# A hybrid decoder layer on one core: two column groups of eight banks become pairs of four banks, with other TensorE work between their matmuls

## The chip, the cores and the metric

The kernel runs on one core of one Trainium2 chip (trn2). The metric is the device time of one execution in microseconds (us), as the median of several runs. TensorE is shortened to PE in the profile, VectorE to DVE, ScalarE to ACT, GpSimd to POOL and SyncE to SP.

## The reference

One layer of a decoder for a prompt of 256 rows and samples of 8 x 4 rows, all float32, 288 rows in all:

```python
x = x + 0.5 * _swiglu(_rmsnorm(x, g_ffn1), w1_gate, w1_up, w1_down)
h = _rmsnorm(x, g_mix)
proj = h @ w_in      # q_a, k_a, v_a, f_a | qk_m (2048), v_m (1024), o_m (1024) | i_m, f_m
...                  # forgetting attention on q_a, k_a, v_a, with cached pages for the samples
qk_c = silu(causal_conv(qk_m))
h_m, C, n, m = _mlstm(q_m, k_m, v_m, i_pre, log_f_m, C0, n0, m0)
y_m = sigmoid(o_m) * _rmsnorm(h_m, g_out_m)
x = x + concatenate([y_a, y_m]) @ w_out
x = x + 0.5 * _swiglu(_rmsnorm(x, g_ffn2), w2_gate, w2_up, w2_down)
```

The output gate o_m is needed only after the mLSTM heads. Besides x, the states and the new keys and values go out.

## The kernel before

Activations lie transposed: a feature tile of 128 on the partitions, the 288 rows along the free axis. Each weight matrix is read once. Each value is split in two float32r parts, and a product of two tiles is three matmuls of 288 columns: hi x hi, lo x hi, hi x lo (L1786 to L1788, "products" below).

Work runs in groups. A group is up to eight column tiles of 128, one in each PSUM bank, summed over all k tiles. The k tiles come in turns of four slots of w_raw, w_hi and w_lo. TensorE takes a turn in two steps, slots 0 and 1, then 2 and 3: each is 48 products at eight banks. SP loads a slot as soon as its last contents are split. ScalarE casts it to w_hi (L632) once TensorE has used that slot of the turn before (w_used), VectorE subtracts for w_lo (L1010), and TensorE waits for w_lo of both slots of a step. At a group's end VectorE drains the banks one by one (banks_free), and the next group's first matmul on a bank waits for that. Each engine has its order written out by hand.

Between products a group can carry other TensorE work in free banks: turn_products calls between(step, b) behind each bank. The group in_a (six banks) does so.

The projection for the mLSTM heads is in_m, four groups of eight banks and four turns: q, k, v, gate. Beside the third and fourth, VectorE computes the causal convolutions (conv, L1543 to L1547, two tiles a turn, two places in conv_acc) and ScalarE their silu (L902):

```python
split_pair(g.turn + 2 * g.turns + (t + 1), 0, width)   # ScalarE, turn t
conv_silu(2 * t)
conv_silu(2 * t + 1)
...
if j >= 2:                                             # VectorE, conv(j)
    dve.wait_ge(sem("conv_used"), 2 * (j - 1))
```

Behind the fourth group comes the heads' preparation: TensorE spreads the samples' decay rows (L2161), transposes v (L1979), two gate rows (L2168) and k (L2186), lays the samples' k and v out by sequence (by_sequence, L2175), computes head 0's scores (L2202 to L2209), transposes the convolution's last rows (L2217), and takes the samples' scores (L2222) and a spread row (L2226). ScalarE and VectorE copy the results out and take the gate's sigmoid (L926). Then the loop over eight heads starts (L2241 is its first matmul). Its states come from DRAM in a ring of four places, two of them slots of w_raw.

The last group is the second half of the second SwiGLU's down projection, down1b: two groups of eight banks and five turns. Behind it, 48 transposes (L2337) turn the result to rows, ScalarE and VectorE copy (L993, L1762), and POOL stores three pieces (L551).

Of the kernel before, what the change touches and what calls it, by code (L numbers as in the profile page):

```python
# [31 lines left out]
F32 = mybir.dt.float32  # L32
# [46 lines left out]
def plan():  # L79
# [17 lines left out]
def build(nc, A, O):  # L97
# [77 lines left out]
    with scope:  # L175
        r_("ym_top", [P, 512])
        ym_hi, ym_lo = r_("ym_hi", [P, H, T], F32R), r_("ym_lo", [P, H, T], F32R)
    right_side, r_ = area("right")
    kmn = r_("kmn", [P, 2, H * HD])
    kms = r_("kms", [P, H * HD])  # L180
    v_seq = r_("v_seq", [P, H, 2, HD])
    C = r_("C", [P, 2, NB, HD])
    Ws, qw, qn = r_("Ws", [SM, H, SM]), r_("qw", [P, H, 2, SM]), r_("qn", [P, H, SM])
    Wt = r_("Wt", [P, 2, 384])
    Cp = r_("Cp", [P, 2, HD])


    kws, vws = qn, Cp[:, :, :].rearrange("p r (h s) -> p (r h) s", s=SM)
    C_ring = [C[:, 0, :, :], C[:, 1, :, :]] + [w_raw[:, i, :].rearrange("p (b e) -> p b e", b=NB) for i in (2, 3)]
# [15 lines left out]
    with scope_mixer:  # L205
# [40 lines left out]
        with scope:  # L246
# [7 lines left out]
            counts = l_("counts", [P, TP])  # L254
            k_sums = l_("k_sums", [P, H, NB])
# [29 lines left out]
    G_A, G_M, G_O = groups["in_a"].index, groups["in_m"].index, groups["out_a"].index  # L285
    OUT_A, OUT_B, OUT_M = groups["out_a"], groups["out_b"], groups["out_m"]
# [24 lines left out]

    def x_final(eng, i, t):
# [4 lines left out]
        else:  # L317
            g = groups["down0b" if i == 1 else "out_m"]
            eng.wait_ge(banks_free, NBANK + g.index * NBANK + t + 1)

# [7 lines left out]
    def _(sp):  # L328
# [18 lines left out]
        def load_swiglu(n):  # L347
# [3 lines left out]
            def down(k0, col):  # L351
                return lambda k: [(0, wd[n][k + k0, :, bass.ds(col, UW)])]
# [14 lines left out]
            g = groups[f"down{n}b"]  # L367
            with sp.Fori(0, 2) as i:
# [28 lines left out]

        def load_out():
# [3 lines left out]
            load_turn(a.turn, range(SLOTS), columns(wo, 0, a.width))  # L402
            load_turn(a.turn + 1, range(2), lambda s: columns(wo, 0, a.width)(SLOTS + s))
# [56 lines left out]
        def state_traffic():  # L460


            sp.wait_ge(banks_free, NBANK + G_O * NBANK)

            def load_state(h):
                sp.dma_start(C_ring[h % 4], A["state_C"][0, :, h, :, :].rearrange("b d e -> d b e")).then_inc(
                    sem(f"C_loaded{h % 4}"), 16)

# [3 lines left out]
            load_state(0)  # L472
# [18 lines left out]
        load_mixer("in_m", 4, wi, COL_M, load_pages)  # L491
# [12 lines left out]
    def _(pool):  # L504
# [79 lines left out]
        pool.wait_ge(banks_free, NBANK + G_O * NBANK)  # L584
        nc.gpsimd.memset(qw[:, :, :, :], 0.0).then_inc(sem("km_ready"), 1)
# [6 lines left out]

        pool.wait_ge(sem("o_sigmoid"), 1)
        for h in range(H):
            pool.wait_ge(sem("sq_ready"), SUM_M + h + 1)
# [7 lines left out]
        for t, n in TT:  # L603
            pool.wait_ge(sem("y_rows_ready"), 2 * (t + 1))
            pool.wait_ge(sem("y_rows_ready_v"), 2 * (t + 1))
            if t < 2:
                store(O["y_prompt"][0, t * P:(t + 1) * P, :], y_rows[:, t, :])
            else:
                store(O["y_sample"].rearrange("b t d -> (b t) d"), y_rows[0:SM, 2, :])
        pool.wait_ge(out_stored, 16 * (6 + 4 + 2 + 3))  # L610
# [1757 lines left out]
```

## Time and profile before

| | |
|---|---|
| runs | 2315.3 us median of 3 (2314.76 to 2317.62) |
| the profiled execution | 2320.72 us, span 2319.1 us |
| TensorE busy | 2290.2 us, 99% |
| VectorE, ScalarE, POOL busy | 53%, 36%, 2% |
| mean granted TensorE clock | 0.994 |
| DMA | 384 MB, 166 GB/s on the mean |

Times in rows are us from the span's start. A timeline row has start, duration, engine, line, operation, output and inputs, and in brackets the idle time before it and who ended it. Matmuls overlap, so the distance of starts tells the pace, not the duration. A plain float32 matmul is counted twice. A windows row has the stretch, its length, then busy us of PE, its weight loads, DVE, ACT and POOL, the granted clock as a share of 2.4 GHz, the DMA share and GB/s.

### The profile page before, as it was taken

How to read it: one execution, taken by the hardware profiler on the slowest of the kernel's cores; microseconds unless marked ns; L12 is line 12 of the kernel's file. 1: busy time of each engine (PE TensorE's matmuls, PEld its weight loads, DVE VectorE, ACT ScalarE, POOL GpSimd, SP SyncE). 2: the span in 40 equal slices, each digit the busy share in tenths (PEclk: the TensorE clock that was granted, in tenths of full speed). 3: DMA queues.
4: the chain of work that ended last, by engine and by line, in shares of the span. 5: the costliest groups of instructions: out<-in, count | busy, mean ns of one | idle time of the engine just before them, and what ended most of it. 6: DMA issues, size and time to landing. Idle time of an engine off the chain costs nothing.

```text
span 2319.1 us, 48002 instructions
## 1 busy us (share of the span) xinstructions
PE 2290.2 (99%) x17805; PEld 2246.8 (97%) x17805; DVE 1228.4 (53%) x1907; ACT 842.8 (36%) x1109; POOL 50.3 (2%) x84
## 2 busy tenths in 40 slices
PE   9999999999999999999999999999999999999998
PEld 8999999999999999887999989999999999999997
DVE  6554444355444455467456766755554434554443
ACT  4333333333333343334334433533333333333332
POOL 2000000000000010010000110000000000000000
PEclk9999999999999999999999999999999999999999
DMA  6555555555554444547445455455554445555443
GB/s 169 180 166 164 164 164 175 166 166 163 171 166 166 165 152 146 168 136 271 157 164 167 132 155 173 151 181 163 163 163 168 171 168 169 168 164 168 164 163 131
DMA packets 176901, 384.05 MB, mean 166 GB/s; under 512 B 19133, under 2 KB 44853, under 8 KB 176501
## 3 DMA queue, kind: packets, MB, share of 16 engines
q1 hardware_dynamic: 173888, 375.99, 50.4%
q0 software_dynamic: 2512, 5.57, 0.8%
q10 hardware_dynamic: 416, 1.32, 0.2%
q8 instruction: 58, 0.95, 0.2%
q14 instruction: 27, 0.22, 0.0%
HBM read 373.09 MB, written 9.70 MB: 165 GB/s over the span
## 4 chain that ended last, share of the span: by engine, by line
PE 95%; DVE 3%; ACT 1%; DMA 0%; issue 0%; SPq 0%; POOL 0%; ACTq 0%; DVEq 0%; POOLq 0%
PE ps L1788 30%; PE ps L1786 30%; PE ps L1787 29%; DVE w_lo L1010 1%; PE ps L2044 1%; DMA w_raw<-in_w_up 0%; ACT w_hi L632 0%; PE ps L2057 0%; PE ps L1856 0%; PE ps L1857 0%; PE ps L1863 0%; PE ps L1990 0%; PE ps L2337 0%; PE ps L1979 0%; PE ps L2245 0%
## 5 line engine op out<-in xcount | busy, mean ns | idle before, releaser
L1010 DVE TENSOR_TENSOR w_lo<-w_raw,w_hi 128x1024 fp32r<-128x1024 f32 (+2 forms) x698 | 789.7, 1172 | 983.9 <-ACT w_hi L632 982.5
L632 ACT CAST w_hi<-w_raw 128x1024 fp32r<-128x1024 f32 (+2 forms) x698 | 670.6, 1008 | 1290.3 <-PE ps L1788 1284.7
L1786 PE MATMUL ps<-x_hi,w_hi 128*128 128x288 f32 (+1 forms) x2752 | 813.0, 295 | 4.4 <-DVE w_lo L1010 2.6
L1788 PE MATMUL ps<-x_hi,w_lo 128*128 128x288 f32 (+1 forms) x2752 | 813.9, 296 | 0.0
L1787 PE MATMUL ps<-x_lo,w_hi 128*128 128x288 f32 (+1 forms) x2752 | 807.7, 293 | 0.0
L1786 PEld LDWEIGHTS ps<-x_hi,w_hi 128*128 128x128 f32 x2752 | 517.5, 188 | 6.3 <-DVE w_lo L1010 3.0
L1787 PEld LDWEIGHTS ps<-x_lo,w_hi 128*128 128x128 f32 x2752 | 521.2, 189 | 0.1
L1788 PEld LDWEIGHTS ps<-x_hi,w_lo 128*128 128x128 f32 x2752 | 516.5, 188 | 0.0
L1786 PE MATMUL ps<-hid_hi,w_hi 128*128 (+1 forms) x1376 | 405.6, 295 | 1.4 <-DVE X L1243 1.4
L1788 PE MATMUL ps<-hid_hi,w_lo 128*128 (+1 forms) x1376 | 407.0, 296 | 0.0
L1787 PE MATMUL ps<-hid_lo,w_hi 128*128 (+1 forms) x1376 | 403.8, 293 | 0.0
L1786 PE MATMUL ps<-xm_hi,w_hi 128*128 128x288 f32 (+1 forms) x896 | 267.6, 299 | 2.5 <-DVE w_lo L1010 2.1
L1788 PE MATMUL ps<-xm_hi,w_lo 128*128 128x288 f32 (+1 forms) x896 | 266.2, 297 | 0.0
L1787 PE MATMUL ps<-xm_lo,w_hi 128*128 128x288 f32 (+1 forms) x896 | 262.1, 293 | 0.0
L1787 PEld LDWEIGHTS ps<-hid_lo,w_hi 128*128 128x128 f32 x1376 | 260.6, 189 | 0.0
L1786 PEld LDWEIGHTS ps<-hid_hi,w_hi 128*128 128x128 f32 x1376 | 258.7, 188 | 1.9 <-DVE X L1243 1.9
L1788 PEld LDWEIGHTS ps<-hid_hi,w_lo 128*128 128x128 f32 x1376 | 258.2, 188 | 0.0
L1786 PEld LDWEIGHTS ps<-xm_hi,w_hi 128*128 128x128 f32 x896 | 168.8, 188 | 7.0 <-DVE w_lo L1010 3.4
L1787 PEld LDWEIGHTS ps<-xm_lo,w_hi 128*128 128x128 f32 x896 | 171.3, 191 | 0.1
L1788 PEld LDWEIGHTS ps<-xm_hi,w_lo 128*128 128x128 f32 x896 | 168.5, 188 | 0.0
L747 ACT ACTIVATE gate<-gate 128x288 f32<-128x288 f32 x86 | 38.3, 445 | 57.5 <-DVE gate L1187 57.5
L1191 DVE TENSOR_TENSOR up<-ps,rsx 128x288 f32<-128x288 f32 x86 | 38.6, 449 | 8.0 <-PE ps L1788 8.0
(487 smaller groups left out, 1438.1 us busy)
## 6 DMA issues: line engine op xcount, KB each, us to landing
w_raw<-in_w_down SPq DMA_DIRECT2D x178, 512.0 KB
w_raw<-in_w_gate SPq DMA_DIRECT2D x320, 256.0 KB
w_raw<-in_w_up SPq DMA_DIRECT2D x320, 256.0 KB
w_raw<-in_w_in SPq DMA_DIRECT2D x64, 512.0 KB
w_raw<-in_w_in SPq DMA_DIRECT2D x64, 384.0 KB
page<-in_cache_k SPq DMA_DIRECT2D x16, 512.0 KB, 4.6
w_raw<-in_w_out SPq DMA_DIRECT2D x16, 512.0 KB
w_raw<-in_w_gate SPq DMA_DIRECT2D x32, 192.0 KB
```

The source lines that it names most:

```text
L632: nc.scalar.copy(w_hi[:, slot, 0:width], w_raw[:, slot, 0:width]).then_inc(w_hi_ready, 1)
L747: nc.scalar.activation(gate[:, j, :], gate[:, j, :], ACT.Silu).then_inc(sem("silu_ready"), 1)
L1010: nc.vector.tensor_tensor(w_lo[:, slot, 0:width], w_raw[:, slot, 0:width], w_hi[:, slot, 0:width].bitcast(F32), ALU.subtract).then_inc(w_l ...
L1191: nc.vector.tensor_tensor(up[:, j, :], ps[:, 2 * j + 1, 0:T], rsx[:, :], ALU.mult).then_inc(banks_free, freed)
L1786: mm(out, hi, x_hi[:, k, :], start=first and pair == 0 and s == slots[0], stop=False)
L1787: mm(out, hi, x_lo[:, k, :], start=False, stop=False)
L1788: ins = mm(out, lo, x_hi[:, k, :], start=False, stop=last and pair == 1 and s == slots[-1])
L2044: ins = tr(ps[:, 5 + 2 * half, i * P:(i + 1) * P], page[:, p % 3, c:c + HD], ident[:, :])
```

## The change

in_m keeps three groups. The gate's 1024 columns become in_o, two groups of four tiles (width 512, four turns each), and the heads' preparation runs between their products in banks 4 to 7. Only scores(0) stays behind them. ScalarE's and VectorE's parts of it are laid out by step. The convolutions move up by a group, to 0, 2, 3, 3 tiles in the turns of the second group and two in each turn of the third. The gate's sigmoid is in two halves, the second behind head 0's exponentials. POOL computes qw. SBUF buffers on the right side get new places, and SP issues the first state load earlier, behind the third turn of in_o's second group.

The second group of down1b becomes down1c, two groups of four tiles and five turns each. Transposes of the eight column tiles already done run between the first one's products, those of the next four between the second one's, and 12 are left behind. The rows go out in nine stores, three of 512 columns at the end from SP and ScalarE. SP's two idle loads at the end are gone.

```diff
@@ -84,9 +84,11 @@
     gate_up_c = [c for j in range(3) for c in (j * P, 384 + j * P)]
     swiglu = [("gu{}c", 1, KD, KD, gate_up_c), ("gu{}a", 5, KD, KD, gate_up), ("down{}a", 2, 24, CHUNK, plain),
               ("gu{}b", 5, KD, KD, gate_up), ("down{}b", 2, 20, 20, plain)]
-    mixer = [("in_a", 4, KD, KD, plain[:6]), ("in_m", 4, KD, KD, plain),
+    mixer = [("in_a", 4, KD, KD, plain[:6]), ("in_m", 3, KD, KD, plain),
+             ("in_o", 2, KD, KD, plain[:4]),
              ("out_a", 1, H, H, plain[:6]), ("out_b", 2, H, H, plain[:5]), ("out_m", 2, H, H, plain)]
-    for n, part in ((0, swiglu), (0, mixer), (1, swiglu)):
+    ending = swiglu[:-1] + [("down{}b", 1, 20, 20, plain), ("down{}c", 2, 20, 20, plain[:4])]
+    for n, part in ((0, swiglu), (0, mixer), (1, ending)):
         for name, count, nk, real, tiles in part:
             out[name.format(n)] = Group(turn, index, nk, real, tiles)
...
@@ SBUF, right side
...
+    kws, vws = (xt[:, i, 0:H * SM].rearrange("p (h s) -> p h s", s=SM) for i in range(2))
+    C_ring = [C0[:, :, :], C1[:, :, :]] + [w_raw[:, i, :].rearrange("p (b e) -> p b e", b=NB) for i in (2, 3)]
     def swiglu_memory(n):
...
+    def conv_tiles(t):
+        first = (0, 0, 2, 5)[t] if t < 4 else 2 * t
+        return range(first, (0, 2, 5, 8)[t] if t < 4 else first + 2)
     def x_final(eng, i, t):
...
@@ SyncE
+        def load_state(h):
+            sp.dma_start(C_ring[h % 4], A["state_C"][0, :, h, :, :].rearrange("b d e -> d b e")).then_inc(
+                sem(f"C_loaded{h % 4}"), 16)
+
         def load_out():
             load_turn(a.turn, range(SLOTS), columns(wo, 0, a.width))
+            sp.wait_ge(w_used, O_MOST)
+            load_state(0)
             load_turn(a.turn + 1, range(2), lambda s: columns(wo, 0, a.width)(SLOTS + s))
             state_traffic()
...
-        for s in range(2):
-            sp.wait_ge(w_loaded[s], 32 * (n_turns + 1))
+        for u in (9, 11):
+            sp.wait_ge(sem("y_rows_ready_v"), u // 2 + 1)
+            sp.dma_start(*y_part(u % 3, 3, 4)).then_inc(sem("y_stored"), 16)
 
 
     SUM_QK, SUM_Y, SUM_M = 0, 16, 24
...
@@ GpSimd
+        for x in qw:
+            nc.gpsimd.memset(x[:, :, :], 0.0).then_inc(sem("km_ready"), 1)
+        pool.wait_ge(sem("km_ready"), H + 2)
+        pool.wait_ge(sem("s_all_ready"), 2)
+        for i in range(2):
+            half = slice(16 * i, 16 * (i + 1))
+            ins = nc.gpsimd.tensor_tensor(qw[i][:, :, half], ext[:, 0:H, TP + 16 * i:TP + 16 * (i + 1)], s_all[:, :, 0, half],
+                                          ALU.mult)
+        ins.then_inc(sem("qw_ready"), 1)
+
         pool.wait_ge(sem("o_sigmoid"), 1)
         for h in range(H):
...
+            pool.wait_ge(sem("y_rows_ready"), (1, 3, 2)[t])
+            pool.wait_ge(sem("y_rows_ready_v"), (2, 1, 3)[t])
+            store(*y_part(t, 0, 2))
+        for t in range(3):
+            pool.wait_ge(sem("y_rows_ready_v" if t == 1 else "y_rows_ready"), (6 + t) // 2 + 1)
+            store(*y_part(t, 2, 3))
+        pool.wait_ge(out_stored, 16 * (6 + 4 + 2 + 6))
+        pool.wait_ge(sem("y_stored"), 3 * 16)
         for b in range(4):
             pool.wait_ge(sem(f"C_stored{b}"), 16 * (H // 4))
         for b in range(2):
...
@@ ScalarE
         for t in range(2 * g.turns):
-            width = UW if t < 2 * g.turns - 1 else OUT_A.width
-            split_pair(g.turn + 2 * g.turns + (t + 1), 0, width)
-            conv_silu(2 * t)
-            conv_silu(2 * t + 1)
-            split_pair(g.turn + 2 * g.turns + (t + 1), 2, width)
...
+        def sigmoid(i):
+            act.wait_ge(banks_free, NBANK + (IN_O.index + i + 1) * NBANK)
+            nc.scalar.activation(om[:, 4 * i:4 * i + 4, :], om[:, 4 * i:4 * i + 4, :], ACT.Sigmoid).then_inc(sem("o_sigmoid"), 1)
+        def conv_rows_copy(b):
+            act.wait_ge(sem("conv_rows_done"), b + 1)
+            nc.scalar.copy(conv_rows[:, b * 512:(b + 1) * 512], ps[0:27, (7, 4, 5, 6)[b], :]).then_inc(sem("conv_rows_ready"), 1)
+        def split_o(step):
+            split_pair(IN_O.turn + step // 2, step % 2 * 2, IN_O.width if step < 16 else OUT_A.width)
+        for step in range(16):
+            if step >= 1:
+                split_o(step + 1)
+            if step == 0:
                 act.wait_ge(sem("conv_used"), 2 * 2 * H)
-            nc.scalar.copy(s_all[:, 4 * b:4 * b + 4, :, :], ps[:, 6 + b, 0:384].rearrange(
-                "p (h r s) -> p h r s", h=4, r=3)).then_inc(sem("s_all_ready"), 1)
-        for i in range(4):
-            act.wait_ge(sem("vT_done"), 6 + i + 1)
-            nc.scalar.copy(vmn[:, i // 2, 4 * (i % 2):4 * (i % 2) + 4, 0:HD],
-                           ps[:, i, :].rearrange("p (h d) -> p h d", h=4)).then_inc(sem("vn_ready"), 1)
-        nc.scalar.activation(om[:, :, :], om[:, :, :], ACT.Sigmoid).then_inc(sem("o_sigmoid"), 1)
-        for i in range(2):
-            act.wait_ge(sem("kmsT_done"), i + 1)
-            nc.scalar.copy(kms[:, i * 512:(i + 1) * 512], ps[:, 4 + i, :]).then_inc(sem("kms_ready"), 1)
...
+            if step == 9:
+                sigmoid(0)
+            if step == 10:
+                act.wait_ge(sem("ws_logits"), 1)
+                nc.scalar.activation(Ws, Ws, ACT.Exp).then_inc(sem("ws_exp"), 1)
+            if step == 15:
+                act.wait_ge(w_used, O_MOST)
+                for i in range(2):
+                    act.wait_ge(sem("kmsT_done"), i + 1)
+                    nc.scalar.copy(kms[:, i * 512:(i + 1) * 512], ps[:, 7 - 2 * i, :]).then_inc(sem("kms_ready"), 1)
+        split_o(17)
         def e_exp(h):
...
+        def y_copy(u):
+            act.wait_ge(sem("y_rows_done"), u + 1)
+            (t, n), q = TT[u % 3], u // 3
+            nc.scalar.copy(y_rows[0:n, t, q * 512:(q + 1) * 512], ps[0:n, 4 + u % 4, :]).then_inc(sem("y_rows_ready"), 1)
+        g = groups["down1c"]
+        for kt in range(1, 2 * g.turns):
+            split_pair(g.turn + kt, 0, g.width)
+            if kt == g.turns + 2:
+                y_copy(6)
+            if kt == g.turns + 3:
+                y_copy(8)
+            split_pair(g.turn + kt, 2, g.width)
+            if kt <= 3:
+                y_copy(2 * kt - 2)
+        y_copy(10)
+        act.wait_ge(sem("y_rows_ready"), 10 // 2 + 1)
+        act.dma_start(*y_part(1, 3, 4)).then_inc(sem("y_stored"), 16)
...
@@ VectorE
@@ -1547,14 +1627,15 @@
                     nc.vector.scalar_tensor_tensor(acc, src, w, acc, ALU.mult, ALU.add).then_inc(sem("conv_done"), 1)
 
         g = groups["in_m"]
-        for i in range(4):
-            if i < 2:
-                split_turns(g, g.turn + i * g.turns, g.turns, UW)
+        for i in range(3):
+            width = UW if i < 2 else IN_O.width
+            if i == 0:
+                split_turns(g, g.turn, g.turns, UW)
             else:
                 for t in range(g.turns):
-                    conv((i - 2) * H + 2 * t)
-                    conv((i - 2) * H + 2 * t + 1)
-                    split_pair(g.turn + i * g.turns + (t + 1), 0, UW if (i, t) != (3, g.turns - 1) else OUT_A.width)
+                    for j in conv_tiles((i - 1) * g.turns + t):
+                        conv(j)
+                    split_pair(g.turn + i * g.turns + (t + 1), 0, UW if t < g.turns - 1 else width)
                     if t < g.turns - 1:
                         split_pair(g.turn + i * g.turns + (t + 1), 2, UW)
...
+        for step in range(16):
+            if step >= 1:
+                split_o(step + 1)
+            if step == 0:
...
+            if step == 6:
+                dve.wait_ge(sem("spread_done"), 2 * H + 1)
...
+            if step == 7:
+                in_o_out(0)
+            if step == 11:
+                dve.wait_ge(sem("ws_exp"), 1)
+                dve.wait_ge(sem("ws_scores"), 1)
...
+            if step == 12:
+                dve.wait_ge(w_used, O_HALF)
+                v_apart(0)
+                k_weighted(0)
+            if step == 13:
+                k_weighted(1)
+                v_apart(1)
+            if step == 14:
+                k_weighted(2)
+                k_weighted(3)
+        in_o_out(1)
+        split_o(17)
...
@@ TensorE
+        def beside_o1(step, b):
+            if step == 0 and b == 2:
+                s_spread()
+            if step == 1 and b < 2:
+                v_natural(b, 4 + b)
+            if step == 2 and b < 2:
+                pe.wait_ge(sem("s_all_ready"), b + 1)
+                v_natural(2 + b, 6 + b)
+            if step == 3 and b < 2:
+                pe.wait_ge(sem("vn_ready"), 6 + b + 1)
+                v_natural(4 + b, 4 + b)
...
+            if step == 6 and b == 0:
+                pe.wait_ge(sem("km_ready"), H)
+                pe.wait_ge(sem("conv_rows_ready"), 1)
+                for h in range(H):
+                    ins = mm(ps[0:SM, 7, h * SM:(h + 1) * SM], ext[:, H + h, TP:T], ext[:, h, TP:T], start=True, stop=True)
+                ins.then_inc(sem("ws_scores"), 1)
+            if step == 6 and b == 1:
+                pe.wait_ge(sem("root_ready"), 2)
+                pe.wait_ge(sem("conv_rows_ready"), 2)
+                mm(ps[:, 4, 0:TP], ones[0:H, :], sq[0:H, 0, 0:H * SM], start=True, stop=True).then_inc(sem("spread_done"), 1)
+        def beside_o2(step, b):
+            if step == 2 and b == 0:
+                pe.wait_ge(sem("vws_ready"), 1)
+                pe.wait_ge(sem("ya_scaled"), 1)
+                by_sequence(vws, 0, 4, "vsT_done")
+            if step == 2 and b == 1:
+                pe.wait_ge(sem("conv_rows_ready"), 3)
+                by_sequence(vws, 1, 5, "vsT_done")
+            if step == 3 and b == 0:
+                pe.wait_ge(sem("conv_rows_ready"), 4)
+                k_natural(0, 6)
+            if step == 4 and b == 0:
+                pe.wait_ge(sem("ws_ready"), 1)
+                k_natural(1, 7)
...
+            if step == 6 and b == 0:
+                pe.wait_ge(sem("kws_ready"), 1)
+                pe.wait_ge(sem("kw_ready"), 2)
+                by_sequence(kws, 0, 7, "kmsT_done")
+            if step == 6 and b == 2:
+                pe.wait_ge(sem("v_seq_ready"), 2)
+                by_sequence(kws, 1, 5, "kmsT_done")
+        for i, beside in ((0, beside_o1), (1, beside_o2)):
+            for kt in range(IN_O.turns):
+                turn_products(IN_O, IN_O.turn + i * IN_O.turns, IN_O.index + i, kt, xm_hi, xm_lo, kt == 0,
+                              kt == IN_O.turns - 1, xr, beside)
...
-                pe.wait_ge(sem("kw_ready"), 2)
+                pe.wait_ge(banks_free, G_O * NBANK + 2)
...
+        def y_transposes(u):
+            (t, n), q = TT[u % 3], u // 3
+            pe.wait_ge(banks_free, (g.index if u < 6 else g.index + 1 if u < 9 else g.index + 2) * NBANK + NBANK)
+            if u >= 4:
+                pe.wait_ge(sem("y_rows_ready" if u % 2 == 0 else "y_rows_ready_v"), (u - 4) // 2 + 1)
             for j in range(4):
-                ins = tr(ps[0:n, i % 4, j * P:(j + 1) * P], X[:, (i % 4) * 4 + j, t * P:t * P + n], ident[:, :])
+                ins = tr(ps[0:n, 4 + u % 4, j * P:(j + 1) * P], X[:, q * 4 + j, t * P:t * P + n], ident[:, :])
             ins.then_inc(sem("y_rows_done"), 1)
+        def beside_first(step, b):
+            if 1 <= step <= 6 and b == 3:
+                y_transposes(step - 1)
+        def beside_second(step, b):
+            if 2 <= step <= 4 and b == 3:
+                y_transposes(step + 4)
+        for i, beside in ((0, beside_first), (1, beside_second)):
+            for kt in range(g.turns):
+                turn_products(g, g.turn + i * g.turns, g.index + i, kt, *mem[1]["hid"], kt == 0, kt == g.turns - 1, hr, beside)
+        for u in range(9, 12):
+            y_transposes(u)
     ctx.close()
```

## Rows read from the trace of the kernel before

**Rows 1.** The page's chain that ended last, share of the span by engine.

```profile
PE 95%; DVE 3%; ACT 1%; DMA 0%; issue 0%; SPq 0%; POOL 0%; ACTq 0%; DVEq 0%; POOLq 0%
```

**Rows 2.** Windows: busy us (x instructions) of each engine, granted clock, DMA.

```profile
1310.82:1317.65 6.83, 6.83 (x36) 5.80 (x34) 2.96 (x8) 4.63 (x8) 0.00 (x0) 0.50 1.15 296
1368.87:1375.70 6.83, 6.83 (x33) 6.68 (x33) 1.84 (x6) 0.42 (x1) 1.30 (x3) 0.50 0.44 135
2303.05:2308.50 5.45, 5.45 (x48) 5.00 (x48) 3.44 (x5) 3.31 (x6) 1.03 (x2) 1.00 0.22 92
```

**Rows 3.** Timeline of TensorE, heads' preparation: start us, us, line, operation.

```profile
1308.42 0.29 PE L1787 MATMUL ps<-xm_lo,w_hi 128*128 128x288 f32 x1
1308.55 0.29 PE L1788 MATMUL ps<-xm_hi,w_lo 128*128 128x288 f32 x1
1309.40 2.46 PE L2161 MATMUL ps<-s_rows,sel 8*128 8x96 f32 x16 [0.55 <-DVE om L1570]
1311.78 5.38 PE L1979 MATMUL ps<-ident,vm 128*128 128x128 f32 x24
...
1317.67 1.06 PE L2175 MATMUL ps<-ident,Cp 128*8 128x128 f32 x32
1318.66 1.97 PE L2186 MATMUL ps<-ident,ext 128*128 128x128 f32 x16
...
1323.29 0.70 PE L2202 MATMUL ps<-ext 128*128 128x256 f32 x2
...
1324.68 1.91 PE L2217 MATMUL ps<-ident,conv_last 128*27 128x128 f32 x16
...
1328.17 0.49 PE L2241 MATMUL ps<-vmn,kmn 128*128 128x129 f32 x2
```

**Rows 4.** Chain that ended last: the third head's scores, start us, us.

```profile
1334.93 0.63 PE ps L2202 x2
```

**Rows 5.** Timelines of ScalarE, then VectorE, in a turn with two convolutions.

```profile
1215.77 1.28 ACT L902 ACT_TABLE_LOAD   x1
1217.06 0.51 ACT L902 ACTIVATE ext<-conv_acc,vecs 128x256 f32<-128x256 f32 x1
...
1220.09 2.00 ACT L632 CAST w_hi<-w_raw 128x1024 fp32r<-128x1024 f32 x2 [1.69 <-PE ps L1788]
1226.43 2.00 ACT L632 CAST w_hi<-w_raw 128x1024 fp32r<-128x1024 f32 x2 [4.34 <-PE ps L1788]
1228.34 0.50 ACT L902 ACTIVATE ext<-conv_acc,vecs 128x256 f32<-128x256 f32 x1
...
1223.45 0.38 DVE L1543 TENSOR_SCALAR conv_acc<-ext,vecs 128x312 f32<-128x312 f32 x1
...
1227.52 2.36 DVE L1010 TENSOR_TENSOR w_lo<-w_raw,w_hi 128x1024 fp32r<-128x1024 f32 x2
```

**Rows 6.** Timeline of TensorE: plain fp32 matmuls between products.

```profile
928.17 0.29 PE L1788 MATMUL ps<-xm_hi,w_lo 128*128 128x288 f32 x1
928.40 1.14 PE L1863 MATMUL ps<-xt,one_hot 128*8 128x288 f32 x4
...
929.71 0.29 PE L1787 MATMUL ps<-xm_lo,w_hi 128*128 128x288 f32 x1
```

**Rows 7.** Timeline of the end of the span, all engines.

```profile
2302.20 0.29 PE L1788 MATMUL ps<-hid_hi,w_lo 128*128 128x288 f32 x1
...
2303.05 5.46 PE L2337 MATMUL ps<-ident,X 128*128 128x128 f32 x48 [0.55 <-DVE X L1243]
...
2308.55 0.68 DVE L1762 COPY y_rows<-ps 32x512 f32<-32x512 f32 x1 [0.19 <-PE ps L2337]
2309.79 0.51 POOL L551 DMA_DIRECT2D out_y_sample<-y_rows  x1 [1.19 <-DVE y_rows L1762]
```

**Rows 8.** DMA issues: queue, count, KB each, median us to landing.

```profile
out_C_prompt<-Cp SPq DMA_DIRECT2D x8, 64.0 KB, 3.1
...
out_y_sample<-y_rows POOLq DMA_DIRECT2D x1, 256.0 KB, 4.5
```

More of the change, by code:

```diff
@@ L285, in build @@
     G_A, G_M, G_O = groups["in_a"].index, groups["in_m"].index, groups["out_a"].index
+    IN_O = groups["in_o"]
+    O_HALF, O_MOST = ((IN_O.turn + IN_O.turns + n) * 2 + 2 for n in (2, 3))
     OUT_A, OUT_B, OUT_M = groups["out_a"], groups["out_b"], groups["out_m"]
@@ L367, in load_swiglu @@
             g = groups[f"down{n}b"]
+            if n == 1:
+                load_group(g, g.turn, down(CHUNK, 0))
+                g = groups["down1c"]
+                with sp.Fori(0, 2) as i:
+                    load_group(g, i * g.turns + g.turn, down(CHUNK, i * g.width + UW, g.width))
+                return
             with sp.Fori(0, 2) as i:
@@ L644, in split_pair, with split_groups @@
             split_hi(turn, s + 1, width)
-        def split_groups(g, n, after, last=False):
+        def split_groups(g, n, after):
             split_turns(g, g.turn, n * g.turns, after)
-            if not last:
-                split_pair(g.turn + n * g.turns, 2, after)
+            split_pair(g.turn + n * g.turns, 2, after)
         def square(i, src):
@@ L945, in _ @@
         e_exp(0)
-        for b in range(4):
-            act.wait_ge(sem("conv_rows_done"), b + 1)
-            nc.scalar.copy(conv_rows[:, b * 512:(b + 1) * 512], ps[0:27, 2 + b, :]).then_inc(sem("conv_rows_ready"), 1)
-        act.wait_ge(sem("ws_logits"), 1)
-        nc.scalar.activation(Ws[:, :, :], Ws[:, :, :], ACT.Exp).then_inc(sem("ws_exp"), 1)
+        sigmoid(1)
         for h in range(H):
@@ L2163, in _, with s_spread @@
-        natural(lambda h, c, n: vm[:, h, c:c + n], 0, "vT_done")
-        pe.wait_ge(sem("rows_exp"), 3)
-        pe.wait_ge(sem("s_all_ready"), 1)
-        for a, row in enumerate((r_row, ws_row)):
-            for t, n in TT:
-                ins = tr(ps[0:n, 6, (3 * a + t) * H:(3 * a + t + 1) * H], row[:, t * P:t * P + n], ident[0:H, 0:H])
-        ins.then_inc(sem("nat_done"), 1)
-        def by_sequence(src, bank, made):
+        def s_spread():
+            pe.wait_ge(banks_free, NBANK + IN_O.index * NBANK)
+            pe.wait_ge(sem("s_rows_ready"), 1)
+            for b in range(2):
+                for j in range(4):
+                    ins = mm(ps[:, 6 + b, j * 96:(j + 1) * 96], sel[0:H, 4 * b + j, :].bitcast(F32), s_rows[:, :, :],
+                             start=True, stop=True)
+                ins.then_inc(sem("s_all_done"), 1)
@@ new lines, in v_natural, with rows_natural @@
+        def v_natural(i, bank):
+            (t, n), half = TT[i // 2], i % 2
+            for j in range(4):
+                ins = tr(ps[0:n, bank, j * P:(j + 1) * P], vm[:, 4 * half + j, t * P:t * P + n], ident[:, :])
+            ins.then_inc(sem("vT_done"), 1)
+        def rows_natural():
+            for a, row in enumerate((r_row, ws_row)):
+                for t, n in TT:
+                    ins = tr(ps[0:n, 6, (3 * a + t) * H:(3 * a + t + 1) * H], row[:, t * P:t * P + n], ident[0:H, 0:H])
+            ins.then_inc(sem("nat_done"), 1)
@@ new lines, in conv_natural, with k_natural, by_sequence @@
+        def conv_natural(i, bank):
+            for j in range(4):
+                ins = tr(ps[0:27, bank, j * P:(j + 1) * P], conv_last[:, 4 * i + j, :], ident[:, :])
+            ins.then_inc(sem("conv_rows_done"), 1)
+        def k_natural(i, bank):
+            for j in range(4):
+                ins = tr(ps[:, bank, j * P:(j + 1) * P], ext[:, H + 4 * (i % 2) + j, i // 2 * P:(i // 2 + 1) * P], ident[:, :])
+            ins.then_inc(sem("kT_done"), 1)
+        def by_sequence(src, i, bank, made):
```

297 lines of the change are left out of this document (156 added, 141 removed).

## The prediction, made before the kernel ran

> **What bounds the kernel now.** I read the page first: the chain that ended last runs through TensorE for 95% of the span [rows 1], and the engine's busy share is 99%. So a change can save only three things: TensorE standing idle, TensorE at its lower clock, and what follows its last instruction. Moving TensorE work from one place to another saves nothing by itself, since it stays on the same engine. I then asked for the granted clock of short windows round the two places that the change touches [rows 2], and last for the order of time there [rows 3 to 7] and the landing times of DMAs [rows 8].
>
> The windows show two stretches of 6.83 us with TensorE busy throughout and a clock of 0.50, the level of 1.2 GHz: one inside the heads' preparation, one behind the heads' loop [rows 2]. What ran before the first was a wait of 0.7 us for the last bank and then matmuls with 8 weight rows (L2161). Each costs 3.4 us.
>
> **The heads' preparation, before.** The last product of the gate's group starts at 1308.55, so the next would be due at 1308.68 (products start 0.13 apart). The heads' loop starts at 1328.17 (L2241) [rows 3]. That is 19.5 us between them. At 2.4 GHz the moved instructions take:
> - 16 matmuls L2161: 2.4 us, 0.9 of it at the lower clock, so 1.9
> - 24 transposes of v (L1979): 48 transposes took 5.47 us [rows 7], 0.114 each, so 2.7. They took 5.3 here
> - six small transposes 0.3
> - four calls of by_sequence: 1.0 for the first (1317.67 to 1318.66) and the same for the last. The 2.74 us from the end of the 16 k transposes (L2186, 1.9 us) to L2202 hold the last and the two for k, so 1.7 for those two, 3.7 in all
> - 16 k transposes 1.8 and 16 of the conv rows 1.8
> - sample scores and the spread of ya's roots, out of the 3.5 us from L2217 to L2241: 0.9
>
> Sum 13.1 us. scores(0) stays where it was: from L2202 at 1323.29 to L2217 at 1324.68, 1.4. So 19.5 is 13.1 + 1.4 + 3.4 of lower clock + some 1.6 of waits.
>
> **The heads' preparation, after.** The 13.1 us now stand between products. What does a switch cost? Two plain fp32 matmuls between products took 1.54 us from the start of the product before to the second one after. Less 2 x 0.13 for the products and 1.07 for themselves, 0.2 is left [rows 6]. Seven pieces of that kind give 1.4. For transposes I take nothing, their engine order is the same as in the stretch of 48. Lower bound of the switches 0, upper 0.2 for each of some 20 pieces, 4.0.
>
> Behind the last product: VectorE must first split 768 columns for two slots and then drain four banks. A pair of 1024 takes ScalarE 2.00 and VectorE ends some 3.4 us behind ScalarE's start [rows 5]. With 768 I estimate 2.9 from the start of the last step, itself 3.2 long, and 0.4 to 0.5 a drain. scores(0) waits for two banks: 0.7 us after the last product. It takes 1.4, and the loop starts at 2.1, since all banks are free at 1.4. Sum after: 13.1 + 1.4 + 2.1 = 16.6. **Gain 19.5 less 16.6, 2.9 us.**
>
> Do the products wait in the new groups? A step is now 24 products, 3.16 us, in place of 6.35. For 512 columns I estimate 1.2 us for ScalarE's two casts and 0.7 for VectorE's last subtraction: half the 1024 rows and a little more [rows 5]. With 0.3 of signal the weights are ready 2.2 us into a step of 3.16 or more. I went through the 16 steps: the longest extra work on either engine (ScalarE's gate for four tiles, with its table 2.4 us; VectorE's v_apart and k_weighted, 1.9) stands in or before steps that inserted work has lengthened by 0.4 to 2 us. I find no wait. What POOL has to do (two memsets, two multiplications) is over some 5 us before the loop asks. The first state load is issued at the end of the fourteenth step, 8 us ahead of the loop; the 256 KB store behind two larger ones landed in 4.5 us [rows 8], so 512 KB should do in well under 8. The second gate's sigmoid now stands on ScalarE between the first and second head, with a table load before and after: 1.3 + 1.1 + 1.3. By my order of time head 1's exponentials end 7.4 us after the last product, and VectorE has multiplied them at 7.9. TensorE asks for them in scores(2), which starts 6.8 us after the loop [rows 3, 4], so at 8.9. Cover 1.0 us, cost nothing.
>
> The Trainium skill (ScalarE: Activation LUTs, section What ACT_TABLE_LOAD costs) gives each switch a drain of 1.38 us on top of the load's 1.28. With two switches TensorE would wait 1.8 us there, and this part's gain would be 1.1. But the activation that follows the load of 1215.77 starts at 1217.06 [rows 5]: 1.28 and no drain, so the sum goes without it.
>
> **The convolutions, moved earlier.** They now stand in two groups, no longer beside the gate's, as 0, 2, 3, 3 tiles in the first one's turns and 2, 2, 2, 2 in the second's. I find the costliest side effect here. Two tiles take VectorE 4.07 us (1223.45 to 1227.52) [rows 5]. Both places of conv_acc are in use, so the third tile of a turn waits for ScalarE's silu of the first. ScalarE's program puts that behind the cast of the next turn's slots 0 and 1, and the cast waits until half of the turn is done. In times from the turn's start (1219.83 in [rows 5]): cast 6.6 to 8.5, silu to 9.2, third conv 9.3 to 11.3, VectorE's two subtractions to 13.6. TensorE wants them at 12.7. So it waits 1.0 us, in two turns. In the second of them the drain of eight banks comes after, and bank 0 is free only 0.5 later: 1.4 us. **Cost 2.4 us.** Lower bound 0, if the order is looser than I read; upper 4, if two waits also shift the turn behind them.
>
> **The last eight column tiles.** Before: the last product starts at 2302.20, the next would be due at 2302.33, and the span ends at 2319.1, 16.8 us later. In it are one drain (to 2303.05), 48 transposes 5.5, the copy of 0.7 from 2308.55, the store issued at 2309.79, landing 4.5 us later at 2314.3 [rows 7, 8], and 4.8 us to the end of the span, which I take as fixed. After: 36 transposes stand between products, nine pieces of 0.44 to 0.46, 4.0 us, still on TensorE. Behind the last product: drain 0.7, 12 transposes, of which the last four end at 2.1, copy from 2.3 to 3.0, a store of 64 KB from SP with 3.1 to land [rows 8] ends at 6.1, then 4.8: 10.9. 16.8 less 10.9 less 4.0: **gain 1.9 us.** Bounds 0.9 (a landing of 4.1) and 2.9 (2.1). The removed dummy loads at the end lie on SP under products and save nothing. Of the ten turns, each step is again 3.16 us against a chain of 2.2; the copies of y rows, 0.6 to 0.7, fit in the 0.9 left and the 0.4 that the inserted transposes add.
>
> **Sum.** 2.9 - 2.4 + 1.9 = 2.4 us off. From the profiled execution's own 2320.7 (span 2319.1): 2318.3. That execution is 5.4 us above the median of the runs, so I carry the difference over: 2315.3 - 2.4 = **2312.9 us**. A change under 0.2% (4.6 us) can't be told from none here.
>
> **The rivals.**
> 1. *No wait in the convolutions' turns.* Against it is the semaphore's order above, for it that TensorE idles nowhere in these groups before. Gain 4.8, time 2310.5. Chance 0.20.
> 2. *The second stretch at 1.2 GHz goes as well,* because the loop's tail falls otherwise in time. For it: it costs 3.4 us [rows 2]; against it: nothing in that tail's work changes. Gain 5.8, time 2309.5. Chance 0.12.
> 3. *The clock falls beside the preparation too.* For it: the 8-row matmuls L2161 preceded the fall, and now the convolutions' waits come close before. Against it: products now surround all of it, and they run at 1.00. The gain of 2.9 becomes -0.5, time 2316.3. Chance 0.12. The Trainium skill (TensorE: Matmul & The Clock Gate, section Part 4: PE-mode transpose) says that transposes don't count as activity for the clock, which would speak for this one. But 48 transposes in a row ran at 1.00 [rows 2].
> 4. *Slower: weights come late in the four-bank groups.* A slot's load is now issued 5 us before its cast is due, where it had some 11. 256 KB landed in 4.5 us behind two larger stores [rows 8], so they should fit, and 1 us of slack lies behind. The price: 18 turns, so 0.1 us late beyond that is 1.8 us. From 0.4 late it turns the sign past 0.2%: 7.2 less 2.4, 2320.1. Chance 0.10.
> My forecast 0.46. Its own range is 2309.5 to 2316.
>
> Faster by over 0.2% (below 2310.7) takes rival 1, rival 2 and a little of the forecast: 0.33. Slower (above 2319.9) is rival 4: 0.10. The rest is 0.57. Range 2307 to 2318: it leaves out rival 4 and the far ends of the others.
>
> **What would show it.** Right: from the last product of the gate to the heads' loop it is 2 to 3 us, with the clock at 1.00 beside the preparation. TensorE idles about 1.0 and 1.4 us in the second and third quarter of the convolutions' first group, released by w_lo. The last product to the span's end is about 11 us. Wrong: idle time of the products on w_lo or on a DMA in each four-bank turn, a clock of 0.50 there, or an end of the span that follows the last landing by other than 4.8 us.

## The result, and the profile after

The changed kernel takes 2320.95 us (median of 14 runs, 2318.02 to 2324.32), the kernel before 2317.59 in as many runs beside it (2314.76 to 2319.6): ratio 1.0018, 95% interval 1.0011 to 1.0025. That is 4.2 us slower (2.5 to 5.8), where I had forecast 2.4 us faster and a range up to 2318. It is just under the 0.2% that I called no change, but the interval leaves zero out, so the sign was wrong. Against the forecast's 2312.9 it is 8.0 us more, and 2.3 of them lie in the starting point: I took the median of 3 runs of the kernel before, 2315.3, where 14 give 2317.59. The profiled execution took 2324.32 us, span 2322.4.

The chain still runs through TensorE, but a DMA now has a share in it (compare [rows 1]).

```profile
PE 94%; DVE 3%; DMA 1%; ACT 1%; issue 1%; SPq 0%; ACTq 0%; DVEq 0%
```

I cut both traces at the same instructions and compared the parts, in us. The first part begins at the last transposes ahead of in_m. Parts 2, 3 and 6 are the change's own. "Lost" is what the lower clock took in parts 1 and 2, summed over slices as (1 - clock) x length.

| part | before | changed | difference |
|---|---|---|---|
| 1: to the gate's last product | 204.3 | 228.5 | +24.2 |
| 2: last product to heads' loop | 19.6 | 2.1 | -17.5 |
| 3: heads' loop to out_a | 44.9 | 44.6 | -0.3 |
| 4: out_a to SwiGLU's last x product | 802.2 | 802.4 | +0.2 |
| 5: from there to the last product | 126.9 | 131.4 | +4.5 |
| 6: last product to the span's end | 16.9 | 10.7 | -6.2 |
| lost to the lower clock in 1 and 2 | 3.4 | 3.4 | 0 |

So the end does what it should, and the front, which was to give 2.9 and take 2.4, costs 6.6. The waits of TensorE on the changed kernel, first in the convolutions' two groups, then round the second group of in_o:

```profile
PE ps L1923 <- DVE ext L1646: 1.3, 1, 1.3
PE ps L1923 <- DVE w_lo L1089: 0.8, 1, 0.8
...
PE ps L1923 <- DVE w_lo L1089: 3.2, 1, 3.2
```

The first two are the convolutions' waits of my step, 2.1 us together. The third I had nowhere. Its place in the timeline (POOL, ScalarE, TensorE):

```profile
1284.60 0.61 POOL L581 DMA_DIRECT2D out_conv_prompt<-conv_rows  x1 [27.59 <-ACT conv_rows L965]
1285.19 0.55 POOL L581 DMA_DIRECT2D out_conv_sample<-conv_rows  x1
1285.73 0.51 POOL L581 DMA_DIRECT2D out_m_prompt<-m_row  x1
1286.23 0.64 POOL L581 DMA_DIRECT2D out_m_sample<-m_row  x1
...
1296.65 0.62 ACT L674 CAST w_hi<-w_raw 128x512 fp32r<-128x512 f32 x1 [5.32 <-DMA w_raw<-in_w_in]
1298.21 1.85 ACT L674 CAST w_hi<-w_raw 128x512 fp32r<-128x512 f32 x3 [0.94 <-DMA w_raw<-in_w_in]
...
1299.61 0.61 PE L1923 MATMUL ps<-xm_hi,w_hi 128*128 128x288 f32 x1 [3.17 <-DVE w_lo L1089]
```

Read it from below: the second group's weights are 3.2 us late because ScalarE waited for two loads of in_w_in, and shortly before, POOL had issued four stores. They used to stand at the heads' loop and came forward together with the conv rows that they wait for. The chain of waits goes the same way: SP issues the load at 1287.01, and it ends at 1298.21.

```profile
1287.01 0.36 SPq L360
1287.67 10.51 DMA w_raw<-in_w_in
1298.21 0.63 ACT w_hi L674
1298.86 0.70 DVE w_lo L1089
```

The windows (columns as in [rows 2]) show what was slow, and what came of it:

```profile
1284.50:1287.00 2.50, 2.50 (x31) 2.30 (x30) 0.98 (x2) 1.14 (x2) 2.27 (x4) 1.00 0.80 243
1287.00:1296.00 9.00, 9.00 (x66) 8.51 (x65) 3.58 (x8) 1.14 (x2) 0.00 (x0) 1.00 0.88 57
1296.00:1299.60 3.60, 0.44 (x4) 0.20 (x2) 1.43 (x3) 2.00 (x4) 0.00 (x0) 0.92 0.62 182
1299.60:1306.10 6.50, 6.49 (x28) 6.50 (x29) 1.19 (x2) 3.18 (x4) 0.00 (x0) 0.52 0.51 156
```

For 9 us the DMA engines are 88% busy and move 57 GB/s, against 243 just before. TensorE idles, and still in the idle time the clock falls to the level of 1.2 GHz. Finer windows, from the same trace:

```profile
1298.00:1299.00 1.00, 0.00 (x0) 0.00 (x0) 0.14 (x1) 0.79 (x2) 0.00 (x0) 1.00 0.52 199
1299.00:1299.60 0.60, 0.00 (x0) 0.00 (x0) 0.60 (x2) 0.59 (x2) 0.00 (x0) 0.51 0.61 85
1299.60:1305.85 6.25, 6.24 (x26) 6.25 (x27) 1.19 (x2) 2.93 (x4) 0.00 (x0) 0.50 0.53 163
1305.85:1307.00 1.15, 1.15 (x22) 0.99 (x25) 0.52 (x1) 1.13 (x3) 0.00 (x0) 1.00 0.00 0
```

The stretch is 6.83 us long, as in [rows 2], and 6.25 of it fall on matmuls: 3.1 us lost. The issues of this stretch, with median us to landing:

```profile
out_conv_sample<-conv_rows POOLq DMA_DIRECT2D x1, 192.0 KB, 2.7
out_conv_prompt<-conv_rows POOLq DMA_DIRECT2D x1, 24.0 KB, 2.1
out_m_prompt<-m_row POOLq DMA_DIRECT2D x1, 0.0 KB, 4.8
out_m_sample<-m_row POOLq DMA_DIRECT2D x1, 0.2 KB, 9.5
```

The large stores land in 2 to 3 us; m_sample, 64 single elements of 4 bytes, needs 9.5.

The heads' part behind the last product (compare [rows 3]), and the end (compare [rows 7]):

```profile
1331.11 0.29 PE L1925 MATMUL ps<-xm_hi,w_lo 128*128 128x288 f32 x1
1331.80 0.70 PE L2418 MATMUL ps<-ext 128*128 128x256 f32 x2 [0.40 <-DVE om L1675]
...
1333.19 0.44 PE L2444 MATMUL ps<-vmn,kmn 128*128 128x129 f32 x2
...
2311.67 0.29 PE L1925 MATMUL ps<-hid_hi,w_lo 128*128 128x288 f32 x1
...
2312.59 1.53 PE L2544 MATMUL ps<-ident,X 128*128 128x128 f32 x12 [0.62 <-DVE X L1884]
...
2314.16 0.68 DVE L1876 COPY y_rows<-ps 32x512 f32<-32x512 f32 x1 [0.18 <-PE ps L2544]
...
2314.86 0.35 SPq L527 DMA_DIRECT2D out_y_sample<-y_rows  x1
```

scores(0) starts 0.7 behind the last product and the loop 2.1, the two figures of the forecast. The end is 10.7 (2322.4 less 2311.67) for 10.9. Two of its terms were off and cancel in part: the last store, issued at 2314.86, lands after 2.4 us where I had 3.1, and the span ends 5.1 behind that landing where I had 4.8.

### The profile page after: what moved, and what is told of

It is laid out like the page before. It is cut to its first block, busy times and chain, and to the rows that moved or that the text cites. A ratio compares the mean times of both kernels' runs of the same rounds, so it can differ in the third digit from the quotient of the medians.

```text
span 2322.4 us, 48173 instructions
## 1 busy us (share of the span) xinstructions
PE 2291.3 (99%) x17805; PEld 2246.5 (97%) x17805; DVE 1230.7 (53%) x1939; ACT 849.1 (37%) x1146; POOL 54.1 (2%) x90
## 4 chain that ended last, share of the span: by engine, by line
PE 94%; DVE 3%; DMA 1%; ACT 1%; issue 1%; SPq 0%; ACTq 0%; DVEq 0%
PE ps L1923 29%; PE ps L1925 29%; PE ps L1924 29%; DVE w_lo L1089 2%; ACT w_hi L674 1%; PE ps L2181 1%; DMA w_raw<-in_w_in 0%; PE ps L2194 0%; DMA x_rows<-in_x_sample 0%; PE ps L1993 0%; PE ps L1994 0%; PE ps L1947 0%; DMA w_raw<-in_w_down 0%; PE ps L2000 0%; PE ps L2127 0%
## 5 line engine op out<-in xcount | busy, mean ns | idle before, releaser
L1089 DVE TENSOR_TENSOR w_lo<-w_raw,w_hi 128x1024 fp32r<-128x1024 f32 (+3 forms) x732 | 792.2, 1123 | 987.8 <-ACT w_hi L674 986.2
L674 ACT CAST w_hi<-w_raw 128x1024 fp32r<-128x1024 f32 (+3 forms) x732 | 673.9, 967 | 1291.4 <-PE ps L1925 1275.5
```

Of the source, the lines that this page charges most:

```text
L674: nc.scalar.copy(w_hi[:, slot, 0:width], w_raw[:, slot, 0:width]).then_inc(w_hi_ready, 1)
L1089: nc.vector.tensor_tensor(w_lo[:, slot, 0:width], w_raw[:, slot, 0:width], w_hi[:, slot, 0:width].bitcast(F32), ALU.subtract).then_inc(w_l ...
```

## The experiments

Ten runs, each timed beside the kernel before. With 11 executions to a kernel (6 for e2) an interval is some 0.001 to either side (2 us), so each verdict below leans on the trace as well. Line numbers shift by a few where lines were added.

**The changed kernel again (e1).** No edit.

> The changed kernel once more, unedited, for a second trace on the chip that the next three share. In the first trace ScalarE's cast waited 5.3 us for a load of in_w_in at 1296.65, TensorE 3.2 us for w_lo behind it, and the clock was 0.50 for the 6.8 us that followed (3.4 us lost): 6.6 us together. If this comes with the kernel, the wait stands here again at the same place, within 1 us of 3.2, and the ratio to the kernel before is 1.001 to 1.0025. If it was a chance delay of one DMA, no such wait is in this trace, and the wait behind the convolutions (0.8 and 1.3 us) is the only new one.

Measured: 2321.76, ratio 1.0019 (1.0010 to 1.0028), TensorE waits 3.3 us at the same place. It is no chance delay. The stretch at the lower clock, which again begins in the idle time, lasts 3.4 us this time, 2.85 of them on matmuls, where it was 6.83 and 6.25.

**The four stores at the heads' loop (e2).**

```diff
-        pool.wait_ge(sem("conv_rows_ready"), 4)
-        store(O["conv_prompt"][0, 0], conv_rows[0:3, :])
...
         pool.wait_ge(w_used, O_MOST)
...
         ins.then_inc(sem("qw_ready"), 1)
+        pool.wait_ge(sem("conv_rows_ready"), 4)
+        store(O["conv_prompt"][0, 0], conv_rows[0:3, :])
...
```

> POOL issues its four stores (conv_prompt 24 KB, conv_sample 192 KB, m_prompt and m_sample in pieces of 4 bytes) behind qw, at the heads' loop, where they stood before the change, in place of between the two groups of in_o. Theory 1, these stores delay the weights' load: TensorE's wait of 3.2 us on w_lo at 1299 is gone, and with it the stretch at clock 0.50 behind it (3.4 us), so that this is up to 6.6 us faster than the changed kernel, ratio to before about 0.999 where the changed one has 1.0018. Theory 2, the four-bank groups give a load too little time whatever else runs: the wait stays within 1 us of 3.2 and the time is the changed kernel's within 1 us. Theory 3, a chance delay: no wait here, but none in the unedited kernel's second trace either.

Measured: 2325.27, ratio 1.0033 (1.0021 to 1.0046), slower still than e1 timed beside it (3.4 us on the mean). The wait for weights is gone, as theory 1 has it, but the delay moved with the stores: they went out at 1318.04 to 1320.31, SP issued the first head's state at 1319.12, it landed 13.2 us later, and TensorE waited for it.

```profile
1332.38 1.08 PE L2453 MATMUL ps<-C,qw 128*32 128x128 f32 x16 [4.51 <-DMA C<-in_state_C]
```

I had expected a faster kernel and not this wait. Here too a load beside the stores comes late, but the rate fell otherwise than in the changed kernel: 221 GB/s over the first 9 us, and 78 over the 4.4 in which TensorE waited. In the kernel before no load ran beside them: SP issued the first four states and no further load until 1339.49 (the kernel before's timeline of SP below), and the stores went out at 1327.79 to 1330.05, between the two.

```profile
1309.37 1.02 SPq L466 DMA_DIRECT2D C<-in_state_C  x2
1311.70 1.76 SPq L466 DMA_DIRECT2D w_raw<-in_state_C  x2
...
1339.49 0.38 SPq L466 DMA_DIRECT2D C<-in_state_C  x1
```

**Silu of the first of three tiles ahead of the cast (e3).**

```diff
+            tiles = conv_tiles(t)
+            early = tiles[:1] if len(tiles) == 3 else tiles[:0]
+            for j in early:
+                conv_silu(j)
             split_pair(g.turn + g.turns + (t + 1), 0, width)
-            for j in conv_tiles(t):
+            for j in tiles[len(early):]:
                 conv_silu(j)
```

> In the two turns with three convolutions ScalarE does the silu of the first tile ahead of the next turn's cast. My step B: the third convolution waits for that silu, TensorE for w_lo 0.8 us and for bank 0 1.3 us in the trace. If that is the cause, both waits go and the time falls by 2.1 us, ratio to before 1.0009 where the unedited one has 1.0018. Rival: VectorE's work of three convolutions and the subtraction (3 x 2.04 + 2.36 = 8.5 us in a turn of 12.7, but only 6.3 behind the cast) is too long by itself: then at least half of the waits stays, over 1 us.

Measured: 2319.11, ratio 1.0005 (0.9996 to 1.0015); neither the 0.8 nor the 1.3 us of wait is in the trace any more. The order on ScalarE was the cause, the rival (too much work for VectorE) falls. The wait for the late load is still there, 3.1 us.

**The end part alone (e4, e10).** The kernel before with down1c, its copies and its stores.

> The kernel before with the last eight column tiles' part of the change alone: down1c, the rows' copies and their stores. My step C: a gain of 1.9 us (the trace of the changed kernel has 10.7 us from the last product to the span's end where I wrote 10.9, and 4.4 for what stands between products where I wrote 4.0, so 1.7): 0.9992 of before. Rival: the 0.3 us of wait for a load seen at 2275 grows in other executions, and the part gives nothing or costs, 1.000 or above.

> The end part alone once more, to narrow its interval and for a second trace: by the steps 16.9 - 10.75 = 6.15 us saved behind the last product and 4.0 given between products, 2.2 us faster, ratio 0.9991; by its first timing 0.9987.

Measured: 2314.28, ratio 0.9987 (0.9978 to 0.9996), and again 2314.15, 0.9988 (0.9979 to 0.9997). In both traces part 5 is 130.9 (4.0 more than before, the forecast's figure) and part 6 is 10.73 to 10.75 (6.15 less): 2.2 us of gain. The timings say 3.0 and 2.8, with intervals that hold 2.2. The rival, a growing wait for a load, did not come: neither trace has one here.

**Which of the stores (e5, e6).** In e5 only m_prompt and m_sample move, forward to in_m's second group; in e6 only the conv rows, back behind the heads' loop, so that the m stores follow the k scaling in POOL's program. The added lines of each (the same lines go at their old place):

```diff
+        pool.wait_ge(sem("conv_used"), 2)
+        store(O["m_prompt"][0].rearrange("b h -> h b"), m_row[:, TP - 1:TP])
+        store(O["m_sample"][0].rearrange("b h -> h b"),
...
         for j in range(H, 2 * H):
```

```diff
+        pool.wait_ge(sem("conv_rows_ready"), 4)
+        store(O["conv_prompt"][0, 0], conv_rows[0:3, :])
+        store(O["conv_sample"][0].rearrange("b r c -> (b r) c"), conv_rows[3:27, :])
         pool.wait_ge(sem("n_rows_ready"), 2)
```

> Only m_prompt and m_sample, 72 pieces of 4 bytes, move ahead of POOL's k scaling, beside in_m's second group, whose loads have an eight-bank turn to land; conv_prompt and conv_sample (216 KB) stay where the change put them. Theory 1a, the 4-byte pieces hold the queue up (m_sample took 9.5 us to land, as long as the load beside it): TensorE's wait of 3.2 to 3.3 us at the start of in_o's second group is gone, under 0.5, and with it the half clock behind it, so 3 to 6.6 us faster than the unedited change, ratio about 1.000. Theory 1b, the 216 KB hold it up: the wait stays at 3 us or more and the ratio at 1.0018. If both share it, the wait is between.

> The mirror of the run before: conv_prompt and conv_sample (216 KB) go behind the heads' loop, m_prompt and m_sample stay beside in_o, and wait no longer for conv_rows but stand behind POOL's k scaling, about 1257, so beside in_o's first group. Theory 1a (4-byte pieces): a wait of TensorE for a load of in_w_in of 2 us or more, now in in_o's first group near 1266 in place of 1299, ratio 1.001 to 1.002. Theory 1b (216 KB): no wait for a load in in_o, ratio about 1.000.

Measured: e5 2318.95, ratio 1.0007 (0.9998 to 1.0016), and no wait for a load in the group at all. The same windows as above, of e5, with the 216 KB of conv rows still issued at 1284.80 and 1285.38:

```profile
1284.50:1287.00 2.50, 2.50 (x31) 2.30 (x30) 0.77 (x2) 1.15 (x3) 1.13 (x2) 1.00 0.81 246
1287.00:1296.00 9.00, 9.00 (x65) 8.51 (x66) 5.08 (x10) 2.28 (x4) 0.00 (x0) 1.00 0.42 127
1296.00:1299.60 3.60, 3.60 (x29) 3.60 (x29) 1.29 (x2) 2.84 (x4) 0.00 (x0) 1.00 0.58 158
```

127 GB/s at 42% busy in place of 57 at 88%, and the clock stays at 1.00. So 216 KB in large pieces cost nothing here. The slow stretch moved with the m stores, which e5 issues at 1178.57 and 1179.13. The same window, of the changed kernel and of e5:

```profile
1183.00:1189.00 6.00, 6.00 (x48) 6.00 (x47) 4.67 (x9) 2.27 (x3) 0.00 (x0) 1.00 0.55 175
1183.00:1189.00 6.00, 6.00 (x48) 6.00 (x47) 4.88 (x9) 2.06 (x3) 0.00 (x0) 1.00 0.91 41
```

91% busy for 41 GB/s in place of 55% for 175, but the turn of eight banks is long enough: TensorE waits for no load.

In e6 (2318.89, ratio 1.0003, 0.9994 to 1.0012) the m stores went out at 1258.59 and 1259.18. The slowdown followed them:

```profile
1256.00:1259.00 3.00, 3.00 (x24) 3.00 (x24) 2.64 (x7) 0.75 (x3) 2.64 (x3) 1.00 0.50 139
1259.00:1268.00 9.00, 9.00 (x64) 8.73 (x63) 4.51 (x11) 3.24 (x6) 0.83 (x2) 0.89 0.63 39
```

39 GB/s for 9 us, with no conv rows under way. So it is the pieces of 4 bytes that slow the loads. But TensorE waited for no load, against my expectation for theory 1a, and neither did ScalarE between 1256 and 1285: the weights had enough slack. That the piece of 2.0 us (the spread of the decay rows) and the v transposes, which lengthen the steps just behind, gave it is argued, not tried. Nor was the changed kernel tried with the m stores alone at 1285, so whether the conv rows beside them add to its wait is not shown.

**All three edits (e7).**

> All three edits: m_prompt and m_sample beside in_m's second group, conv_prompt and conv_sample behind the heads' loop, the silu of the first of three tiles ahead of the cast. If the stores (up to 6.6 us in the first trace) and the convolutions' waits (2.1 us) are all that the forecast lacked, the front part gives its 2.9 us and the end its 1.9: 4.8 us under the kernel before, ratio 0.998 or less. If something else in the front part costs, the ratio stays at that of the end part alone, 0.9987, or above.

Measured: 2317.01, ratio 0.9999 (0.9990 to 1.0008). No wait for loads or convolutions is left, and it still stands 0.0012 above the end alone. The 0.998 of both parts lies outside its interval, so the front part as designed does not give its 2.9 us. In its trace the lower clock is beside the preparation, behind the spread of the decay rows (2.02 us from 1258.89, 16 matmul records with 8 weight rows):

```profile
1258.70:1261.70 3.00, 3.00 (x24) 2.74 (x24) 0.53 (x3) 0.96 (x2) 0.00 (x0) 1.00 0.55 175
1261.70:1265.10 3.40, 3.40 (x17) 3.38 (x16) 1.70 (x4) 1.73 (x3) 0.00 (x0) 0.52 0.13 22
```

Of the eight traces with the preparation beside products and the spread in one piece, four (e3, e6, e7, e9) have such a stretch of about 3.4 us, beginning some 3 us after the spread began, and four (the changed kernel, e1, e2, e5) don't. They are not spread evenly: the three with the silu moved ahead (e3, e7, e9) all have it, and of the five without only e6. No run was made to tell whether that edit brings it.

**The spread in two pieces (e8).**

```diff
-            if step == 0 and b == 2:
-                s_spread()
+            if step == 0 and b in (1, 2):
+                s_spread(b - 1)
```

> The mended kernel with the eight matmuls that spread the samples' decay rows (8 weight rows each) in two pieces of four, behind the second and the third bank of in_o's first step, in place of one piece of 2.0 us. In three traces (e3, e6, e7) the clock was 0.50 for some 3.4 us from 2.6 to 3.1 us after that piece began, in three (the changed kernel, e1, e5) it was not. Theory 1, the piece's length brings it: none here, and 1 us faster on the mean than the mended kernel, ratio about 0.9995. Theory 2, the fall is set by something outside of the piece, or half the piece is enough: it stays as frequent, ratio 0.9999, and this trace may have it.

Measured: 2316.55, ratio 0.9996 (0.9987 to 1.0005). Its trace has no lower clock there:

```profile
1258.00:1270.00 12.00, 12.00 (x92) 11.48 (x92) 5.36 (x13) 6.15 (x11) 0.00 (x0) 1.00 0.30 89
```

It has the silu moved ahead too, so it stands against three traces with a lower clock there. But it is one trace, and 0.0003 less than e7 is inside the intervals: inconclusive.

**The front part alone, with the three edits (e9).**

> The front part of the change (in_o, the preparation beside it, the convolutions moved up) with all three edits of the mended kernel, and the end as in the kernel before. Forecast by my steps: 2.9 us faster than before, ratio 0.9987. By the runs so far (mended 0.9999, end alone 0.9987): 2.8 us slower, 1.0012. By the traces' stages at the full clock (mended 221.88 us from in_m's start to the heads' loop, before 220.55): 1.3 us slower, 1.0006, plus or minus what the lower clock takes in either.

Measured: 2318.71, ratio 1.0002 (0.9993 to 1.0012), 0.4 us slower. My steps' 0.9987 lies outside the interval. The 1.0012 that I took from the difference of two runs is at its edge; the sum at the full clock, 1.0006, fits.

The end part alone has the lowest ratio of all, in both its timings, and its interval lies below 1.

## Why the prediction was wrong

**The end (step C in the expectations above): right.** 4.0 between products in e4 and e10 (4.5 in the first trace, with a wait of 0.3 for late weights), 10.7 for 10.9 behind them, where a shorter landing (2.4 for 3.1) made up for a later copy and a longer tail. Gain 2.2 for 1.9 forecast.

**The convolutions (step B there): right.** Two waits, at 1193.8 and 1208.1, behind the two turns with three tiles, 0.8 and 1.3 us for the 1.0 and 1.4 of the forecast, with the cause it named: e3 shows it. (These are the third and fourth turns of the group. The forecast's list of signs says second and third quarter, which its own step does not give.)

**The loop's start and the sigmoid: right.** 2.07 to 2.08 us in every trace with in_o for 2.1, and no wait for the second sigmoid. Its cover of 1.0 us held: the part from loop to out_a is no longer than before (44.6 for 44.9).

**The moved work: 1 us too cheap.** In e8, where no wait and no lower clock is left, part 1 takes 219.96, so 15.6 more than before (204.33), for 13.1 + 1.4 forecast. The transposes cost what I said (0.44 a piece of four). The other 1.1 us stand in the plain fp32 pieces and the small transposes: one by_sequence takes 1.19 (from the product at 1299.50 to the second one after, at 1300.95, less two products), where I had 0.93 and 0.2 for the switch, and the six small transposes take 0.6 for 0.3. At the full clock the front is thus 1.3 (e7) to 1.5 us (e8) longer than before, where I had 0.5.

**The step that failed first: "I find no wait".** I walked through the 16 steps with each engine's work and checked the state load, but of POOL I counted only "two memsets, two multiplications". Its four stores, which wait for conv_rows and so were pulled into in_o by the moved transposes, I left out, so the wait stood in the sum at nothing. They cost 3.1 to 3.3 us of waiting and behind it 1.4 (e1) to 3.1 us (first trace) of lower clock. e5 takes both away in its trace; its ratio is 0.0012 (2.8 us) lower than that of e1, with intervals that overlap. Rival 4 had the right symptom, weights late in a four-bank group, and the right size of slack, but the wrong form: 0.1 late in each of 18 turns and not once 3.2, and without the cause.

**The second: "3.4 of lower clock" as a saving.** I read the whole 6.83 us of [rows 2] as the price of the place. The same code lost only 1.7 us there in e4 and in e10. And the preparation took the stretch along: behind the spread, four traces of eight lost 1.7 us, so 0.85 on the mean. That is rival 3, in half of the traces and at half of its price. The saving is some 1.4 us (2.3 on the mean of three traces less 0.85), not 3.4, and an estimate from few traces: with the silu moved ahead, where three of three have the stretch behind the spread, it is 0.6. The unprofiled runs do not settle it, for they differ in sign: the mean clock of e9's runs is 0.9959 where the kernel before beside it has 0.9951, 1.9 us of the span less, and e7's is 0.9958 where the end alone has 0.9962, 0.9 us more. Rival 2 (the stretch behind the loop goes too) occurred in one trace, e3; in the others 1.7 or 3.4 us stayed there.

The Trainium skill (DMA: Bandwidth & Descriptors, section Specifications) says that transfers under 512 B are done as read-modify-write, and its Rules for kernel authors that a strided last dimension becomes one descriptor per element. The second agrees with e5's trace, where POOL's queue has 64 packets between 1180 and 1183, as many as m_sample has elements. No run here shows the first. In e5 these packets are over before the slow stretch of 1183 to 1189, though the store lands only 9.0 us after its issue, so by which way they slow the other queue stays open.

**The sum anew, by the traces:** front at the full clock +1.3, lower clock -1.4, convolutions +2.1, the m stores' wait 3.3 and 1.4 to 3.1 behind it, the end -2.2. That is 4.5 to 6.2 slower, where 4.2 (2.5 to 5.8) was measured. The upper end goes with the first trace, the slowest of the 14 runs. The front alone is 0.1 faster by this sum, where e9 measured 0.4 slower.

**Open:** what decides whether the clock falls behind the spread, whether two pieces avoid it, and how pieces of 4 bytes slow the loads of another queue.

## What to carry to other kernels

When a step moves forward, follow every instruction that waits for its result, on the idle engines too: a store that was harmless beside one stage can starve the loads of another, and shrinking a group's loads to half leaves half the slack. Judge a store by its pieces and not by its bytes; put the element-wise ones where loads have a whole long turn. And don't book a stretch at the lower clock as a saving of the place where one trace has it: look at a second trace, and at whether the work that precedes it moves along.

## What was not expected of the hardware

Behind 72 pieces of 4 bytes on POOL's queue all DMA together moved 39 and 57 GB/s for 9 us, with the engines 63% and 88% busy (e6 and the changed kernel), while in e5 216 KB in large pieces landed in under 3 us and delayed nothing. It does not always look so: in e2 the engines moved 221 GB/s for 9 us behind the same stores and only then fell to 78. A stretch at 1.2 GHz is not always 6.83 us long: the same program had 3.4 and 6.83 us round the same wait, and e4 3.4 us where [rows 2] have 6.83. And it does not wait for TensorE's next matmul: round the late load it began while the engine still idled, so 0.6 us of it cost nothing.
